# Moving an 8-byte tile so that activations and split weights start at multiples of 64 bytes

## The chip, the cores and the metric

One core of one Trainium2 chip runs one program, a transformer-like pair of blocks. The metric is the device time of one execution in microseconds (us). TensorE (PE) does the matmuls, its weight loads are the profile's PEld; VectorE is DVE, ScalarE is ACT, GpSimd is POOL, SyncE is SP. "Moving" is the operand that streams through TensorE (512 columns), "weights" is the 128x128 operand that is loaded before it.

## What is computed

Two blocks on x of shape 1 x 1024 x 1024. Block one: modulation from `c`, `h @ w_in`, three mixers (a state-space scan, a Fourier mix, window attention), `@ w_out`, then `(gelu(gate) * val) @ w_down` with a width-3 convolution after `w_up`. Block two: `u @ w_in_2`, four branches, a gated merge, `@ w_out_2`, then a squared-ReLU MLP. In cut form:

```python
h = rms_norm(x, g_pre_mix[l]) * (1.0 + sc_m) + sh_m
z = h @ w_in[l]
...
up = dwconv3(h @ w_up[l], conv_w[l], conv_b[l])
y = (jax.nn.gelu(gate) * val) @ w_down[l]
...
proj = jnp.einsum("btd,dp->btp", u, w_in[l])
hid = jnp.square(jax.nn.relu(jnp.einsum("btd,df->btf", u, w_up[l])))
m = jnp.einsum("btf,fd->btd", hid, w_down[l])
```

## The kernel before, in words

Activations lie transposed, channels on the 128 partitions and 1024 positions along each. The large products are done in split precision: every fp32 number is held as a high and a low part in type fp32r, and each product of a 128x128 weight block with 512 positions takes three matmuls, high by high, high by low, low by high. They are at lines 1698 to 1700 (function `mm`) for the plain products and at 1732 to 1734 (`pair_mm`) for two MLP stages in which pairs of panels are combined so that seven products do for eight; the merge of the four branches has the same three at 2078 to 2080. There are 2368 + 840 + 128 of each, so 10008 such matmuls of 128x512 in all.

Weights come as panels of 128x1024. A DMA brings a panel into the raw buffer `wraw` (line 1249), ACT copies it to the high part (helper line 2918), POOL subtracts to get the low part (helper line 3448). The split panel goes to one of four slots, and the slots are used in turn (`take_slot`: panel n goes to `(n + self.shift) % NW`, `NW` is 4). Three slots are one tile, `whl`, the fourth is a tile of its own, `whl4`, since it is allocated later:

```python
        A = sb("act", [P, 2, NK, T], F32R)
        wraw = sb("wraw", [P, NRAW, 1024])
        whl3 = sb("whl", [P, NW - 1, 2, 1024], F32R)
        sel = sb("sel", [P, 2])
...
        whl4 = sb("whl4", [P, 2, 1024], F32R)
        whl = [whl3[:, n, :, :] for n in range(NW - 1)] + [whl4[:, :, :]]
```

The moving operand is `act` (both parts of the normed activations) in the products with `w_in`, `w_out`, `w_up`; `hid1` or `hid2` (both parts of the MLP's hidden layer) in those with `w_down`; in the paired stages `act` and the sums `t12`, `t3`, `t3t` of halves of it. Profiles leave numbers out of tile names: `whl` stands for `whl` and `whl4`, `hid` for both hidden tiles, `t` for `t12` and `t3`. `sel` holds two columns and is read by 32 small matmuls in the first 50 us (lines 1756 and 1775).

The allocator puts a tile of 8 bytes per partition into 32 bytes. So the tiles lie as follows in each partition, by the built programs:

| tile | start before | over a multiple of 64 | start after | over a multiple of 64 |
|---|---|---|---|---|
| sel | 117728 | 32 | 19424 | 32 |
| act | 19424 | 32 | 19456 | 0 |
| wraw | 84960 | 32 | 84992 | 0 |
| whl (slots 0 to 2) | 93152 | 32 | 93184 | 0 |
| whl4 (slot 3) | 117760 | 0 | 117760 | 0 |
| hid1, hid2 | 158720 | 0 | 158720 | 0 |
| t12, t3, t3t | 125952, 191488, 158720 | 0 | the same | 0 |
| hz2, z3, wbl (the merge's operands) | 158720, 191488, from 224512 | 0 | the same | 0 |

All parts and blocks inside these tiles are at multiples of 512 bytes from their start (256 in the merge), so an operand has the remainder of its tile. Below, a matmul is **mixed** when its moving operand and its weights have different remainders (32 and 0, or 0 and 32), and **equal** when they have the same one. Counted from the program before:

| moving | weights | matmuls | kind |
|---|---|---|---|
| act | whl | 5160 | equal (32, 32) |
| act | whl4 | 1752 | mixed |
| hid1, hid2 | whl | 1248 | mixed |
| hid1, hid2 | whl4 | 384 | equal (0, 0) |
| t12, t3, t3t | whl | 840 | mixed |
| t12, t3, t3t | whl4 | 240 | equal (0, 0) |
| merge | merge | 384 | equal (0, 0) |

That makes 3840 mixed and 6168 equal ones. By time of start in the profiled execution, mixed and equal:

| stretch, us | mixed | equal |
|---|---|---|
| 0 to 420 | 120 | 441 |
| 420 to 552 | 144 | 379 |
| 552 to 670 | 240 | 248 |
| 670 to 940 | 513 | 660 |
| 940 to 1000 | 159 | 76 |
| 1000 to 1160 | 372 | 320 |
| 1160 to 1300 | 201 | 300 |
| 1300 to 2100 | 651 | 2469 |
| 2100 to 2400 | 641 | 651 |
| 2400 to 2700 | 733 | 563 |
| 2700 to the end | 66 | 61 |

Of the kernel before, what the change touches and what calls it, by code (L numbers as in the profile page):

```python
# [14 lines left out]
P = 128  # L15
# [19 lines left out]
class Marks:  # L35
# [35 lines left out]
    def mark(self, name, *key):  # L71
        return self.up(1, name, key)
# [4 lines left out]
    def done(self, name, *key):  # L77
        if self.known:
            return self.sem(name), self.value[(name, *key)]
        return self.sem(name), 0  # L80
# [1149 lines left out]
def build(nc, t):  # L1230
    ctx = ExitStack()
    with ctx:
        def sb(name, shape, dt=F32, c=ctx, side=None):
            return c.enter_context(nc.sbuf_tensor(name, list(shape), dt, side=side))
# [10 lines left out]
        gmod = sb("gmod", [P, 6, 8])  # L1245
        r8 = sb("r8", [P, NG])
        halfpi = sb("halfpi", [P, 1])
        A = sb("act", [P, 2, NK, T], F32R)
        wraw = sb("wraw", [P, NRAW, 1024])
        whl3 = sb("whl", [P, NW - 1, 2, 1024], F32R)  # L1250
        sel = sb("sel", [P, 2])


        cp = ExitStack()
# [88 lines left out]
        crow = X[1][:, 7, :]  # L1343
        XA = A[:, 0, :, :].bitcast(F32)
        arow = {j: tmp0[1 - j][:, :] for j in range(2)}
# [112 lines left out]
        def hid_view(name, q, h):  # L1458

            n = HID_SLOT[name][h]  # L1460
            if n > 5:
                return A[:, 1, 2 * (n - 6) + q, :]
            return H["f1"][:, n, q, :] if name == "f1" else hid[:, n, q, :]

        def part_view(s, t, q, e):

            if t == "t4":
                return A[:, q, e, 512:1024]
            if t == "t3":
                return TX3[:, 4 * q + e, :] if 4 * q + e < 6 else TX3t[:, 4 * q + e - 6, :]  # L1470
            return TX12[:, 0 if t == "t1" else 1, q, e, :]
# [6 lines left out]
        def moving(s, b, q, e):  # L1478

            if b[0] == "t":  # L1480
                return part_view(s, b, q, e)
            return A[:, q, e + (0 if b == "b11" else 4), HALF[b == "b22"]]

# [174 lines left out]
        def tensor(pe):  # L1658
# [12 lines left out]
            def mm(i, k0, k1):  # L1671
# [13 lines left out]
                for e in range(k0, k1):  # L1685
# [10 lines left out]
                    hi, lo = (whl[plan.slot[n]][:, q, cols[e]:cols[e] + 128] for q in range(2))  # L1696
                    x_hi, x_lo = (hid_view(g.kind[:2], q, k)[:, c] if down else A[:, q, k, c] for q in range(2))
                    pe.matmul(PSB[g.bank][:, :], hi, x_hi, start=e == 0, stop=False)  # L1698
# [394 lines left out]
        def vector(v):  # L2093
# [9 lines left out]
            def stt(out, a, s, b, op0, op1):  # L2103
                return v.scalar_tensor_tensor(out=out, in0=a, scalar=s, in1=b, op0=op0, op1=op1)  # L2104
# [55 lines left out]
            def apply(s, half):  # L2160
# [10 lines left out]
                for j in range(9):  # L2171
# [10 lines left out]
                    if j:  # L2182
                        i = j - 1
                        if shift is not None:
                            w.wait_ge(*done("apA", s, half, i))
                            stt(A[:, 1, i, c], tm[i % nt], shift(i), A[:, 0, i, c].bitcast(F32), ALU.add,
                                ALU.subtract).then_inc(*mark("apD", s, half, i))
# [1849 lines left out]
```

How the kernel before makes its waits and increments, by code:

```python
    def wait_ge(self, sem, value):  # L98
        if self.met.get(sem.name, 0) < value:
            self.met[sem.name] = value
            self.engine.wait_ge(sem, value)
# [1560 lines left out]
            def start():  # L1662
                w.wait_ge(*done("ones"))
# [7 lines left out]
            def mm(i, k0, k1):  # L1671
                g = tiles[i]
                n, down = g.n, g.kind in EVAC_ON_DVE
                w.wait_ge(*done("hi", n))
                w.wait_ge(*done("lo", n))
                if g.free and k0 == 0:
                    w.wait_ge(*done(*g.free))
                if down:
                    c0, k = chunk_of[g.kind][g.chunk]
                    cols, ks = [(g.pos * k + e) * 128 for e in range(k)], [c0 + e for e in range(k)]
                else:
                    ks = K_OUT if g.kind == "w_out" else range(8)
                    cols = [128 * k for k in ks]
                c = HALF[g.half]
                for e in range(k0, k1):
                    k = ks[e]
                    if down:
                        w.wait_ge(*hid_done(g.kind[:2], k))
                    elif g.kind == "w_out":
                        for d in mixed_done(k):
                            w.wait_ge(*d)
                    elif g.kind == "w_out2":
                        w.wait_ge(*split_done(g.half, k))
                    else:
                        w.wait_ge(*apply_done(APPLIED[g.kind], g.half, k))
                    hi, lo = (whl[plan.slot[n]][:, q, cols[e]:cols[e] + 128] for q in range(2))
```

## Time and profile before

| what | value |
|---|---|
| three runs | 2754.02, 2754.8, 2760.42 us; the median is 2754.8 |
| span of the profiled execution | 2751.9 us (the median of the runs is 2.9 us above it) |
| PE matmul busy | 2637.7 us, 96% of the span, 12542 records |
| DVE, ACT, POOL busy | 53%, 37%, 40% |
| granted TensorE clock | 0.93 to 420 us, then 0.99 to 1.00 to the last slice |

The profile gives no time of its own for the profiled execution beyond the span; the runs are timed around it. A matmul's duration is longer than the distance to the next start, since matmuls overlap, so rate is read from distances of starts, or from how many lie in a stretch.

### The profile page before, as it was taken

What the parts mean: (1) busy time and instruction counts of PE and PEld (TensorE: products, weight loads), DVE (VectorE), ACT (ScalarE), POOL (GpSimd) and SP (SyncE); (2) the same over time, 40 slices, a digit from 0 to 9 for tenths busy, and PEclk for the clock granted to TensorE, in tenths of its full rate; (3) what the DMA queues carried; (4) which work ended last, traced back from release to release, by engine and by line L of the source; (5) the groups of instructions that cost most, each with busy time, mean ns of one, the idle gap of its engine ahead of it and who ended that gap; (6) DMA issues with size and microseconds to landing.
All of it is one profiled execution on the core that took longest, in us unless ns stands there. A gap on an engine that the chain in (4) does not pass through costs nothing.

```text
span 2751.9 us, 31627 instructions
## 1 busy us (share of the span) xinstructions
PE 2637.7 (96%) x12542; PEld 2080.4 (76%) x12542; DVE 1465.6 (53%) x1881; ACT 1029.3 (37%) x1600; POOL 1091.4 (40%) x605
## 2 busy tenths in 40 slices
PE   6889989999999999999999999999999999999997
PEld 2657757777888788877777788888788788888885
DVE  5646658797777722276766422433457655322225
ACT  4413655455444511345454321211354434312112
POOL 1322114256656544442211142322353655534443
PEclk8999999999999999999999999999999999999998
DMA  6453247321222343241123122111324233433322
GB/s 247 178 146 101 78 173 285 113 81 66 81 84 83 112 146 126 84 145 59 54 68 109 54 88 67 58 48 48 137 91 153 77 115 104 149 118 128 115 77 85
DMA packets 109619, 297.92 MB, mean 108 GB/s; under 512 B 13344, under 2 KB 28192, under 8 KB 109472
## 3 DMA queue, kind: packets, MB, share of 16 engines
q1 hardware_dynamic: 102592, 275.36, 29.4%
q10 hardware_dynamic: 3456, 10.73, 1.0%
q0 software_dynamic: 3424, 9.81, 0.9%
q8 instruction: 100, 1.64, 0.2%
q14 instruction: 47, 0.39, 0.1%
HBM read 233.09 MB, written 62.76 MB: 108 GB/s over the span
## 4 chain that ended last, share of the span: by engine, by line
PE 71%; DVE 5%; ACT 1%; issue 1%; POOL 1%; DMA 1%; POOLq 0%; SPq 0%; DVEq 0%; ACTq 0%
PE ps L1698 16%; PE ps L1700 15%; PE ps L1699 15%; PE ps L1732 5%; PE ps L1734 5%; PE ps L1733 5%; PE pc L1732 1%; PE pc L1734 1%; PE pc L1733 1%; PE pss L2026 1%; PE pc L2078 1%; PE pc L2080 1%; PE pc L2079 1%; POOL whl L3448 1%; DVE pad L2104 0%
## 5 line engine op out<-in xcount | busy, mean ns | idle before, releaser
L3448 POOL TENSOR_TENSOR whl<-wraw,whl 128x1024 fp32r<-128x1024 f32 (+2 forms) x309 | 648.0, 2102 | 1242.0 <-ACT whl L2918 1241.8
L1698 PE MATMUL ps<-act,whl 128*128 128x512 f32 x1824 | 735.5, 403 | 34.7 <-DVE act L2098 9.2
L1699 PE MATMUL ps<-act,whl 128*128 128x512 f32 x1824 | 718.0, 394 | 0.0
L1700 PE MATMUL ps<-act,whl 128*128 128x512 f32 x1824 | 717.5, 393 | 0.0
L1698 PEld LDWEIGHTS ps<-act,whl 128*128 128x128 f32 x1824 | 344.9, 189 | 134.9 <-issue 43.3
L2918 ACT ACTIVATE whl<-wraw 128x1024 fp32r<-128x1024 f32 (+2 forms) x309 | 268.1, 869 | 461.9 <-PE ps L1700 372.6
L1700 PEld LDWEIGHTS ps<-act,whl 128*128 128x128 f32 x1824 | 344.9, 189 | 76.9
L1699 PEld LDWEIGHTS ps<-act,whl 128*128 128x128 f32 x1824 | 345.3, 189 | 75.7 <-issue 4.1
L2098 DVE TENSOR_TENSOR y<-y,ps 128x512 f32<-128x512 f32 x176 | 120.9, 687 | 365.6 <-PE ps L1700 365.4
L1698 PE MATMUL ps<-hid,whl 128*128 128x512 f32 x544 | 216.8, 399 | 4.4 <-DVE y L2502 4.3
L1700 PE MATMUL ps<-hid,whl 128*128 128x512 f32 x544 | 214.4, 394 | 0.0
L1699 PE MATMUL ps<-hid,whl 128*128 128x512 f32 x544 | 214.1, 394 | 0.0
L1732 PE MATMUL ps<-act,whl 128*128 128x512 f32 x360 | 141.2, 392 | 1.9 <-ACT rl L2918 1.3
L1734 PE MATMUL ps<-act,whl 128*128 128x512 f32 x360 | 140.9, 391 | 0.0
L1733 PE MATMUL ps<-act,whl 128*128 128x512 f32 x360 | 140.7, 391 | 0.0
L1698 PEld LDWEIGHTS ps<-hid,whl 128*128 128x128 f32 x544 | 102.1, 188 | 31.2 <-DVE y L2502 6.4
L1732 PE MATMUL ps<-t,whl 128*128 128x512 f32 x300 | 118.6, 395 | 3.0 <-ACT pad L2918 3.0
L1700 PEld LDWEIGHTS ps<-hid,whl 128*128 128x128 f32 x544 | 102.1, 188 | 24.5
L1699 PEld LDWEIGHTS ps<-hid,whl 128*128 128x128 f32 x544 | 102.0, 188 | 24.2 <-issue 0.7
L1734 PE MATMUL ps<-t,whl 128*128 128x512 f32 x300 | 118.3, 394 | 0.0
L2098 DVE TENSOR_TENSOR sgm<-sgm,pc 128x512 f32<-128x512 f32 x48 | 32.7, 681 | 154.5 <-PE pc L2080 154.5
L2918 ACT ACTIVATE sgm<-ps 128x512 f32<-128x512 f32 x46 | 27.5, 597 | 231.3 <-PE ps L1700 223.0
(402 smaller groups left out, 4206.1 us busy)
## 6 DMA issues: line engine op xcount, KB each, us to landing
wraw<-in_w_in SPq DMA_DIRECT2D x63, 512.0 KB, 3.4
wraw<-in_f1u SPq DMA_DIRECT2D x72, 256.0 KB, 2.8
wraw<-in_f2d SPq DMA_DIRECT2D x36, 512.0 KB, 3.4
wraw<-in_w_out SPq DMA_DIRECT2D x32, 512.0 KB, 3.4
x<-in_w_ada SPq DMA_DIRECT2D x32, 512.0 KB, 7.2
hid<-hscr SPq DMA_DIRECT2D x29, 512.0 KB, 6.6
xs<-y SPq DMA_DIRECT2D x24, 512.0 KB, 6.3
wraw<-in_f2u SPq DMA_DIRECT2D x48, 256.0 KB, 3.3
```

Source lines behind the costliest of these rows:

```text
L1698: pe.matmul(PSB[g.bank][:, :], hi, x_hi, start=e == 0, stop=False)
L1699: pe.matmul(PSB[g.bank][:, :], hi, x_lo, start=False, stop=False)
L1700: m = pe.matmul(PSB[g.bank][:, :], lo, x_hi, start=False, stop=e == len(ks) - 1)
L1732: pe.matmul(o[:, :], hi[:, c], x_hi, start=k in OPENS and e == 0, stop=False, skip_group_check=True)
L1733: pe.matmul(o[:, :], hi[:, c], x_lo, start=False, stop=False, skip_group_check=True)
L1734: m = pe.matmul(o[:, :], lo[:, c], x_hi, start=False, stop=e == 3, skip_group_check=True)
L2026: m = pe.matmul(PSS[:, h, n * 128:n * 128 + 128], ks[pr, cs_], qs[pr, cs_], start=True, stop=True)
L2078: pe.matmul(PSC[half][:, :], wh, yh, start=e == 0, stop=False)
L2079: pe.matmul(PSC[half][:, :], wh, yl, start=False, stop=False)
L2098: return v.tensor_tensor(out, a, b, op)
L2918: return a.activation(out, in_, func, **kw)
L3448: return g_.tensor_tensor(out, a, b, op)
```

## The change

`sel` is allocated before `act` instead of after `whl`. It takes the 32 bytes there, so `act`, `wraw` and `whl` start 32 bytes later, and everything allocated after them stays where it was. No size, no instruction and no order changes on any engine.

```diff
@@ -1245,10 +1245,10 @@
         gmod = sb("gmod", [P, 6, 8])
         r8 = sb("r8", [P, NG])
         halfpi = sb("halfpi", [P, 1])
+        sel = sb("sel", [P, 2])
         A = sb("act", [P, 2, NK, T], F32R)
         wraw = sb("wraw", [P, NRAW, 1024])
         whl3 = sb("whl", [P, NW - 1, 2, 1024], F32R)
-        sel = sb("sel", [P, 2])
 
 
         cp = ExitStack()
```

Since profiles leave tile numbers out, two pieces of PE's order (the same in both kernels) tell which slot a matmul reads. The first is where the panel in slot 2 ends and the one in slot 3 begins, 48 matmuls before the first merge matmul (L2078):

```order
5893 L1699 MATMUL ps0<-act,whl 128x512
5894 L1700 MATMUL ps0<-act,whl 128x512
5895 L1698 MATMUL ps1<-act,whl4 128x512
5896 L1699 MATMUL ps1<-act,whl4 128x512
...
5942 L1700 MATMUL ps0<-act,whl4 128x512
5943 L2078 MATMUL pc0<-z3 128x512
```

The second is in the last `w_down` product, where slot 3 with 48 matmuls stands between others, and 102 matmuls from slots 0 to 2 follow, the last 6 of them the first of a panel whose matmuls alternate between `hid2` and `act`:

```order
9166 L1700 MATMUL ps2<-hid2,whl 128x512
9167 L1698 MATMUL ps3<-hid2,whl4 128x512
...
9214 L1700 MATMUL ps2<-hid2,whl4 128x512
9215 L1698 MATMUL ps3<-hid2,whl 128x512
...
9316 L1700 MATMUL ps3<-hid2,whl 128x512
9317 L1698 MATMUL ps3<-act,whl 128x512
```

Nothing in either piece moves; only the addresses behind `act` and `whl` do.

## Rows read from the trace of the kernel before

**Rows 1.** The page: span, busy time, PE and its granted clock by slice.

```profile
span 2751.9 us, 31627 instructions
...
PE 2637.7 (96%) x12542; PEld 2080.4 (76%) x12542; DVE 1465.6 (53%) x1881; ACT 1029.3 (37%) x1600; POOL 1091.4 (40%) x605
...
PE   6889989999999999999999999999999999999997
...
PEclk8999999999999999999999999999999999999998
```

**Rows 2.** Waits of PE, the longest entry: waited for, us in total, times, longest us.

```profile
PE ps L1766 <- DMA adaw<-in_w_ada: 10.0, 9, 2.7
```

**Rows 3.** The page's groups: busy us, mean ns of one, idle before.

```profile
L1698 PE MATMUL ps<-act,whl 128*128 128x512 f32 x1824 | 735.5, 403 | 34.7 <-DVE act L2098 9.2
L1699 PE MATMUL ps<-act,whl 128*128 128x512 f32 x1824 | 718.0, 394 | 0.0
```

**Rows 4.** Timeline of PE, 1605 to 1628 us: start us, duration us, instruction.

```profile
1605.34 0.39 PE L1698 MATMUL ps<-act,whl 128*128 128x512 f32 x1
...
1616.22 0.39 PE L1698 MATMUL ps<-act,whl 128*128 128x512 f32 x1
...
1627.41 0.39 PE L2078 MATMUL pc<-z 128*128 128x512 f32 x1
```

**Rows 5.** Timeline of PE, 2385 to 2441 us.

```profile
2385.16 0.39 PE L1698 MATMUL ps<-hid,whl 128*128 128x512 f32 x1
...
2396.05 0.39 PE L1698 MATMUL ps<-hid,whl 128*128 128x512 f32 x1
...
2418.45 0.39 PE L1698 MATMUL ps<-hid,whl 128*128 128x512 f32 x1
...
2440.74 0.39 PE L1698 MATMUL ps<-hid,whl 128*128 128x512 f32 x1
```

**Rows 6.** Groups of PE, 2168.8 to 2171.2 us: t12 with whl.

```profile
L1732 PE MATMUL ps<-t,whl 128*128 128x512 f32 x4 | 1.6, 395 | 0.0
```

**Rows 7.** Groups of PE, 2248.7 to 2250.1 us: t3 with whl4.

```profile
L1732 PE MATMUL ps<-t,whl 128*128 128x512 f32 x3 | 1.2, 389 | 0.0
```

**Rows 8.** Windows of PE: stretch, length, busy (matmuls), clock, DMA share, GB/s.

```profile
0.00:420.00 420.00, 352.75 (x2233) 0.93 0.48 155
420.00:552.00 132.00, 129.18 (x565) 1.00 0.53 196
552.00:670.00 118.00, 113.84 (x490) 1.00 0.22 72
670.00:940.00 270.00, 269.94 (x1173) 1.00 0.23 82
...
1000.00:1160.00 160.00, 160.00 (x693) 1.00 0.32 115
1160.00:1300.00 140.00, 132.88 (x591) 0.99 0.30 104
...
2100.00:2400.00 300.00, 298.67 (x1293) 1.00 0.34 118
2400.00:2700.00 300.00, 300.00 (x1297) 1.00 0.29 105
```

**Rows 9.** The chain that ended last, by line, 560 to 680 us.

```profile
by line: POOL whl L3448 8.3%; PE ps L1732 7.8%; DVE pad L2098 7.7%; DVE pad L2104 7.6%; PE ps L1734 7.4%; PE ps L1733 7.3%; issue 5.5%; DVE cv L2104 5.0%; DMA hscr<-pad 4.7%; DVE act L2098 4.4%; DVE x L2104 4.0%; DVE late L2098 3.8%; ACT pa
```

**Rows 10.** The same, 1160 to 1300 us.

```profile
by line: PE ps L1698 17.3%; PE ps L1700 16.5%; PE ps L1699 16.4%; DMA E<-in_hmask 3.8%; issue 3.7%; POOL whl L3448 3.5%; DVE pad L2104 3.0%; PE pc L1983 2.5%; DVE act L2098 2.4%; DMA wraw<-in_w_in 2.4%; ACT act L2918 2.3%; DVE z L2098 2.2%;
```

**Rows 11.** Timeline of POOL, 1607 to 1648 us: low parts of four successive panels.

```profile
1607.16 2.39 POOL L3448 TENSOR_TENSOR whl<-wraw,whl 128x1024 fp32r<-128x1024 f32 x1 [8.29 <-ACT whl L2918]
1618.04 2.41 POOL L3448 TENSOR_TENSOR whl<-wraw,whl 128x1024 fp32r<-128x1024 f32 x1 [8.49 <-ACT whl L2918]
...
1629.24 2.41 POOL L3448 TENSOR_TENSOR whl<-wraw,whl 128x1024 fp32r<-128x1024 f32 x1 [2.67 <-ACT whl L2918]
...
1645.62 2.41 POOL L3448 TENSOR_TENSOR whl<-wraw,whl 128x1024 fp32r<-128x1024 f32 x1 [9.11 <-ACT whl L2918]
```

## The prediction

> **What bounds the kernel now.** I read the page first. PE's matmuls are busy in 2637.7 of 2751.9 us, no other engine in more than 53%, and after the first slices every slice of PE is a 9 at a granted clock of 9 or 10 tenths, that is at 2.4 GHz [rows 1]. Its waits are few: the longest entry comes to 10 us over the whole program [rows 2]. So the time is the number of matmuls times the distance between two starts, wherever PE is on the chain. The next question is that distance. The page's groups cannot give it, because a matmul's duration (394 or 403 ns [rows 3]) overlaps the next one. From starts it can be had, and here the program holds an experiment of its own: the weight slot changes from panel to panel while everything else stays.
>
> With `act` moving, 48 matmuls on a panel in slot 2 (remainders 32 and 32) take 1616.22 - 1605.34 = 10.88 us, which is 226.7 ns each; the next 48, the same line and tiles but slot 3 (32 and 0), take 1627.41 - 1616.22 = 11.19 us, 233.1 ns each [rows 4]. That alone could be something about slot 3. But with `hid` moving it is the other way round: slot 3 (0 and 0) takes 2396.05 - 2385.16 = 10.89 us for 48, 226.9 ns each, and the 96 from slots 0 and 1 (0 and 32) take 22.40 us, 233.3 ns each [rows 5]. The paired stage agrees by durations, which grow with the distance: `t12` with `whl` has 395 ns, `t3` with `whl4` 389 [rows 6, 7]. So neither tile is slow by itself. A matmul costs some 6.5 ns more (233.3 - 226.8) when moving operand and weights lie at different remainders over 64 bytes, and both equal kinds, 32/32 and 0/0, have the same speed.
>
> **The change, term by term.** It adds and removes no instruction. It makes all 10008 of these matmuls equal, at 0 and 0.
>
> 1. The mixed matmuls get faster: 3840 x 6.5 ns = 25.0 us.
>
> 2. A surcharge where the kind changes. Between 2418.45 and 2440.74 us a panel in slot 2 and one in slot 3 are used with `hid` and `act` in turns of six, so 48 of 96 matmuls are mixed. They should take 96 x 230.05 ns = 22.08 us and take 22.29 [rows 5]: 0.2 us, or 4.4 ns per mixed one, on top. Over the four long stretches with PE alone the windows tell the mean. 670 to 940, 1000 to 1160, 2100 to 2400 and 2400 to 2700 us are 1030 us with 1028.6 busy and 1173 + 693 + 1293 + 1297 matmuls [rows 8], less one at most edges that is counted on both sides: 4453. At 226.75 ns they would take 1009.7 us; the 2259 mixed ones add 14.7; 1.4 us are idle; 4.2 us remain, 1.9 ns per mixed matmul. Scaled to 3840 that is 7.1 us. I take all of it, as no kind changes after the edit; if it has another cause it stays, so the bounds are 0 and 7.1. Terms 1 and 2 make 32.1 us, or 8.4 ns per mixed matmul.
>
> 3. What is not passed on. In 0 to 420 us PE is busy 84% [rows 8] and waits for transfers and small steps; 120 mixed ones are worth 1.0 us, and I take it as lost. In 420 to 552 us PE is busy 98%, 144 are worth 1.2 us, half lost. In 552 to 670 us 240 are worth 2.0 us, but PE's three lines are only 22.5% of the chain there, beside POOL's splits and DVE's `pad` work [rows 9]: 1.6 lost. In 1160 to 1300 us 201 are worth 1.7 us with PE 53% of the chain [rows 10]: 0.8 lost. For the scattered waits elsewhere I add 0.2. Together 4.2 us. The bounds are 0 (all passed on) and about twice this, 8.
>
> 4. The other engines. POOL's low-part subtraction is 2.39, 2.41, 2.41 and 2.41 us on four successive panels [rows 11], one of which goes to `whl4` while it reads `wraw` at remainder 32; the target's remainder makes no difference there. I take nothing for DVE, ACT and POOL, and should a write get slower by some ns, PE covers it: POOL sat idle 8 us and more before three of those four. The raw panels' transfers end early enough for that too. If this cover were gone, a late split would show as waits of PE on `whl`, of which it has none near the 10 us of its longest entry now [rows 2]. `sel` keeps its remainder.
>
> Sum: 25.0 + 7.1 - 4.2 = 27.9 us. From the span of 2751.9 that gives 2724.0; the median of the runs is 2.9 above the span, so 2726.9, said as 2727 us, 1.0% less. A difference of 0.3% (8.3 us) is about what a measurement of this kernel can tell from none.
>
> **A rule that speaks against it.** The rows show a distance that depends on both operands' addresses. The Trainium skill, page "SBUF — State Buffer", section "SBUF: two separate sides", gives TensorE its own port and, in the table under "A bandwidth-pool intuition that's wrong", a second independent read port for weight loads; its specifications name lines of 16 bytes. By that a start 32 bytes off is still on a line's edge and the two reads cannot meet, and the time would stay at 2754.8. The two crossing stretches [rows 4, 5] disagree with it, by 6.5 ns a matmul.
>
> **Rivals.**
>
> A. The remainder is not the cause. The two slots could differ in something else that goes with it, such as how far apart the operands lie, and both tiles that are now at 32 would simply keep their mixed partners slow. Then nothing changes: 2754.8. Against it: act, hid and t cross over with the slot, far apart in address, and after the edit every operand has the relation that `hid` and `whl4` have now. For it: remainders have been seen in two values only, and each with few tiles. The page's rule above ends at the same time. Chance 5%.
>
> B. Real on PE, but eaten by others. If a faster PE finds DVE and the splits late in the paired stages too, where DVE is busiest, half of terms 1 and 2 goes: 2754.8 - 16 = 2738.8, say 2739. For it: the chain of 560 to 680 us. Against it: 670 to 940 us has the same paired work and PE is busy 269.94 of 270 us [rows 8]. Chance 12%.
>
> C. Slower. While PE waits, the granted clock can fall: in 0 to 420 us, busy 84%, it is 0.93, which is 59 us at 1.2 GHz, and in stretches of 96% and more it is 1.00 [rows 8]. If shorter matmuls leave more gaps, gaps bring falls and each us at 1.2 GHz costs half a us. To end above no change by 0.3% this must cost 28 + 8 = 36 us, so 72 us more at half clock, over twice what there is now; the result would be 2763. [...] Chance 1%.
>
> **How the numbers follow.** The forecast has 82%. Its own range is from all passed on (2754.8 - 32.1 = 2722.7, and 2 us below that for a run like the fastest and for a last matmul rate a little under 226.7) to no surcharge gained and doubled losses (25.0 - 8 = 17: 2737.8). With B and some room for the median of few runs, which reached 5.6 us above itself once, the range is 2719 to 2741; A and C, 6%, and some ends of the others are outside. Faster by over 0.3% are the forecast and B, 94% with a little of A's doubt taken off: 0.93. Within 0.3%: 0.05. Slower: 0.02.
>
> **What would show it.** In the profile after, 48 matmuls on any slot take 10.88 to 10.90 us with any moving tile; the durations are 389 ns everywhere, with L1699's mean under 392; 300 us of pure matmuls hold about 1323 instead of 1293 to 1297; PE's busy total falls by 30 us or more, while its waits rise by some 4. DVE, ACT and POOL keep their busy times. The prediction is wrong if panels of slot 3 still differ from the others, if all matmuls are now at 233 ns (then 32/32 was the good case, and equal at 0 fails with the new neighbours), or if PE's idle time grows by more than 8 us.

## The result and the profile after

| | median, us | runs | against before, 95% interval |
|---|---|---|---|
| before | 2756.9 | 2754.02 to 2760.42 | |
| changed | 2732.6 | 2729.13 to 2737.33 | 0.991 [0.9896, 0.9925] |
| predicted | 2727 | 2719 to 2741 | |

The kernel is 24 us faster (27.9 forecast). The forecast was worked out from the 2754.8 us of three runs; with a fourth run the median of the kernel before is 2756.9. The page of the changed kernel:

```profile
span 2727.3 us, 31627 instructions
...
PE 2613.6 (96%) x12542; PEld 2082.2 (76%) x12542; DVE 1460.0 (54%) x1881; ACT 1028.4 (38%) x1600; POOL 1095.9 (40%) x605
...
PEclk8999999999999999999999999999999999999998
```

Beside [rows 1] the span is 24.6 us shorter and PE's busy time 24.1, with the same granted clock in every slice; the other engines keep theirs within 6 us. PE's unbusy time is the same: 2751.9 - 2637.7 = 114.2 and 2727.3 - 2613.6 = 113.7. The two groups of [rows 3], busy us and mean ns of one:

```profile
L1698 PE MATMUL ps<-act,whl 128*128 128x512 f32 x1824 | 732.3, 401 | 35.1 <-DVE act L2098 8.3 <-POOL act L3448 6.6 <-DVE act L2104 5.3
L1699 PE MATMUL ps<-act,whl 128*128 128x512 f32 x1824 | 714.5, 392 | 0.0
```

The timeline of PE (start us, duration us) answers to [rows 4]: the panel in slot 2 begins at 1594.86, the one in slot 3 at 1605.74, and the merge at 1616.70. The next panel in slot 3 is from 1665.66 to 1676.54.

```profile
1594.86 0.39 PE L1698 MATMUL ps<-act,whl 128*128 128x512 f32 x1
...
1605.74 0.44 PE L1698 MATMUL ps<-act,whl 128*128 128x512 f32 x1
...
1616.70 0.39 PE L2078 MATMUL pc<-z 128*128 128x512 f32 x1
...
1665.66 0.39 PE L1698 MATMUL ps<-act,whl 128*128 128x512 f32 x1
...
1676.54 0.39 PE L2078 MATMUL pc<-z 128*128 128x512 f32 x1
```

Slot 2 still takes 10.88 us for 48 matmuls, 226.7 ns each. Slot 3 takes 10.96 the first time, where its first matmul was held up a little (0.44 instead of 0.39 us), and 10.88 the second, where it took 233 ns a matmul before. The same for [rows 5], slot 3 and then slots 0 and 1 with `hid`, and then the panels that alternate between `hid` and `act`:

```profile
2367.44 0.39 PE L1698 MATMUL ps<-hid,whl 128*128 128x512 f32 x1
...
2378.32 0.39 PE L1698 MATMUL ps<-hid,whl 128*128 128x512 f32 x1
...
2400.08 0.39 PE L1698 MATMUL ps<-hid,whl 128*128 128x512 f32 x1
...
2421.84 0.39 PE L1698 MATMUL ps<-hid,whl 128*128 128x512 f32 x1
```

48 matmuls in 10.88 us, 96 in 21.76 and 96 in 21.76: all 226.7 ns. The alternating stretch had 22.29 us, so the surcharge there is gone too. Windows of PE (length, busy and number of matmuls), beside [rows 8]:

```profile
552.00:670.00 118.00, 112.19 (x488) 1.00 0.21 72
670.00:940.00 270.00, 269.64 (x1190) 1.00 0.24 84
1000.00:1160.00 160.00, 159.92 (x708) 1.00 0.34 120
2100.00:2400.00 300.00, 298.61 (x1309) 1.00 0.32 113
```

15 to 17 more matmuls fit into each of the three long stretches. In 552 to 670 us there are 488 where there were 490: no gain there.

### The profile page after: what moved, and what is told of

Its sections match the earlier page's. It is cut to its first block, busy times and chain, and to the rows that moved or that the text cites. A ratio compares the mean times of both kernels' runs of the same rounds, so it can differ in the third digit from the quotient of the medians.

```text
span 2727.3 us, 31627 instructions
## 1 busy us (share of the span) xinstructions
PE 2613.6 (96%) x12542; PEld 2082.2 (76%) x12542; DVE 1460.0 (54%) x1881; ACT 1028.4 (38%) x1600; POOL 1095.9 (40%) x605
## 4 chain that ended last, share of the span: by engine, by line
PE 70%; DVE 5%; POOL 2%; ACT 1%; issue 1%; DMA 1%; SPq 0%; POOLq 0%; DVEq 0%; ACTq 0%
PE ps L1698 15%; PE ps L1700 15%; PE ps L1699 15%; PE ps L1732 5%; PE ps L1734 5%; PE ps L1733 5%; PE pc L1732 1%; PE pc L1734 1%; PE pc L1733 1%; PE pss L2026 1%; POOL whl L3448 1%; PE pc L2078 1%; PE pc L2080 1%; PE pc L2079 1%; DVE pad L2104 0%
## 5 line engine op out<-in xcount | busy, mean ns | idle before, releaser
L1698 PE MATMUL ps<-act,whl 128*128 128x512 f32 x1824 | 732.3, 401 | 35.1 <-DVE act L2098 8.3
L1699 PE MATMUL ps<-act,whl 128*128 128x512 f32 x1824 | 714.5, 392 | 0.0
L1700 PE MATMUL ps<-act,whl 128*128 128x512 f32 x1824 | 714.3, 392 | 0.0
L1698 PEld LDWEIGHTS ps<-act,whl 128*128 128x128 f32 x1824 | 344.8, 189 | 132.1 <-issue 38.5
L1700 PEld LDWEIGHTS ps<-act,whl 128*128 128x128 f32 x1824 | 344.9, 189 | 73.4
L1699 PEld LDWEIGHTS ps<-act,whl 128*128 128x128 f32 x1824 | 345.4, 189 | 72.5 <-issue 4.1
L1698 PE MATMUL ps<-hid,whl 128*128 128x512 f32 x544 | 214.4, 394 | 0.4
L1700 PE MATMUL ps<-hid,whl 128*128 128x512 f32 x544 | 212.2, 390 | 0.0
L1699 PE MATMUL ps<-hid,whl 128*128 128x512 f32 x544 | 212.0, 390 | 0.0
L1732 PE MATMUL ps<-act,whl 128*128 128x512 f32 x360 | 140.6, 390 | 3.4 <-ACT whl L2918 1.5
L1698 PEld LDWEIGHTS ps<-hid,whl 128*128 128x128 f32 x544 | 102.4, 188 | 24.5 <-DVE y L2502 1.8
L1732 PE MATMUL ps<-t,whl 128*128 128x512 f32 x300 | 117.0, 390 | 2.9 <-ACT pad L2918 2.9
L1699 PEld LDWEIGHTS ps<-hid,whl 128*128 128x128 f32 x544 | 102.3, 188 | 22.0 <-issue 1.0
L1700 PEld LDWEIGHTS ps<-hid,whl 128*128 128x128 f32 x544 | 102.2, 188 | 21.4
```

The costliest lines, as they stand in the source:

```text
L1699: pe.matmul(PSB[g.bank][:, :], hi, x_lo, start=False, stop=False)
L1700: m = pe.matmul(PSB[g.bank][:, :], lo, x_hi, start=False, stop=e == len(ks) - 1)
L1732: pe.matmul(o[:, :], hi[:, c], x_hi, start=k in OPENS and e == 0, stop=False, skip_group_check=True)
```

## The experiments

All kernels differ from the changed one only in where tiles lie, so they compute the same. Where an edit adds lines ahead of the matmuls, their line numbers are one or two higher; the text says which is which. **d** is the start of the moving operand less the start of the weights.

### Is it the remainder over 64?

All at 32, from the order of before:

```diff
         whl3 = sb("whl", [P, NW - 1, 2, 1024], F32R)
         sel = sb("sel", [P, 2])
+        sb("pad32", [P, 8])
```

> The order of before (act at 32 over a multiple of 64) and a further tile of 32 bytes behind sel, so that whl4, hid, t12, t3 and the merge's tiles lie at 32 too: all 10008 matmuls equal, none at a multiple of 64. If it is the relation of the two operands that counts, this runs like the changed kernel, 24 to 28 us under before (about 2730), and every matmul starts 226.7 ns after the last. If starts at multiples of 64 are what is fast, it is slower than before, up to 10008 x 6.5 ns = 65 us over the changed kernel (2797).

Measured: 2750.7 us, 0.9984 of before [0.9974, 0.9994]. This is neither of the two numbers expected. All pairs have equal remainders over 64, and yet it gains 6 us and not 24. This was the first sign that the reading of the traces was too narrow.

`sel` between `act` and `wraw`:

```diff
-        sel = sb("sel", [P, 2])
         A = sb("act", [P, 2, NK, T], F32R)
+        sel = sb("sel", [P, 2])
         wraw = sb("wraw", [P, NRAW, 1024])
```

> sel stands between act and wraw: act at 32, all weights, hid and sums at 0. By the relation, 6912 matmuls (all with act) are mixed at 233.3 ns and the 3096 others equal at 226.7: 6912 x 6.6 = 46 us over the changed kernel and some us for changes of kind, so about 2780, 20 to 25 us over before. If slot 3 itself, or the number of tiles at multiples of 64, decides, it lies between before and the changed kernel (2732 to 2757), since more tiles are at 0 than before.

Measured: 2769.5 us, 1.0049 of before [1.0032, 1.0065]. More tiles lie at multiples of 64 than before, and it is slower: slot 3 or the number of round addresses is ruled out as the cause. The rise over the changed kernel is 37 us where 46 and more were expected.

64 bytes behind `act`:

```diff
         A = sb("act", [P, 2, NK, T], F32R)
+        sb("pad64", [P, 16])
         wraw = sb("wraw", [P, NRAW, 1024])
```

> 64 bytes are put behind act, so act is at 0 and everything behind it at 64 over a multiple of 128. If only the remainder over 64 counts, it runs like the changed kernel (about 2730). If the remainder over 128 counts, 6912 matmuls are mixed and it runs near 2780.

Measured: 2766.7 us, 1.0035 of before [1.0022, 1.0048]. Every tile starts at a multiple of 64, and the kernel is 34 us slower than the changed one. So "a multiple of 64" is not what makes it fast. The groups of line 1699 (1700 in the last kernel), with 32 and with 64 bytes between `act` and the weights:

```profile
L1699 PE MATMUL ps<-act,whl 128*128 128x512 f32 x1824 | 726.3, 398 | 0.0
...
L1699 PE MATMUL ps<-hid,whl 128*128 128x512 f32 x544 | 213.0, 391 | 0.0
```

```profile
L1700 PE MATMUL ps<-act,whl 128*128 128x512 f32 x1824 | 725.5, 398 | 0.0
...
L1700 PE MATMUL ps<-hid,whl 128*128 128x512 f32 x544 | 212.7, 391 | 0.0
```

In both, the `act` group's mean is 6 ns above the changed kernel's 392 while `hid`, which kept its relation to the weights, has 391.

### Ladders of distances

Since slots change from panel to panel, one kernel can hold four distances for `act` and four for `hid`. In the near ladder the slots are 32 bytes apart:

```diff
-        whl3 = sb("whl", [P, NW - 1, 2, 1024], F32R)
+        whl3 = sb("whl", [P, 6168], F32R)
...
-        whl4 = sb("whl4", [P, 2, 1024], F32R)
-        whl = [whl3[:, n, :, :] for n in range(NW - 1)] + [whl4[:, :, :]]
+        whl4 = sb("whl4", [P, 2048], F32R)
+        sb("padC", [P, 8])
+        whl = [t_.rearrange("p (q c) -> p q c", q=2) for t_ in [whl3[:, 2056 * n:2056 * n + 2048] for n in range(NW - 1)] + [whl4[:, 0:0 + 2048]]]
```

> A ladder read in the trace, not meant to be fast. act at 0; weight slots 0 to 3 at 0, 32, 64 and 96 over a multiple of 512; hid, sums and merge tiles at 128. With d for start of the moving operand less start of the weights, over a multiple of 512, act gives d of 0, -32, -64, -96 and hid gives 128, 96, 64, 32. If d alone decides (both tiles' own places do not), the spacing seen so far must come back: 0 -> 226.7 ns, -32 -> 233.3, -64 -> 233.3, 32 -> 233.3, 64 -> 229.0; -96, 96 and 128 are new. If the places themselves decide, at least one of these five comes out otherwise by over 1 ns.

PE's timeline in the near ladder. The plain triple (the three matmuls of one product, L1698 to L1700 in the changed kernel) begins at L1699 here. `act` with slots at 32, 64 and 96 begins at 1603.07, 1614.27 and 1625.47, and with the one at 0 at 1642.19; the merge begins at 1636.70 and 1653.09:

```profile
1603.07 0.39 PE L1699 MATMUL ps<-act,whl 128*128 128x512 f32 x1
...
1614.27 0.40 PE L1699 MATMUL ps<-act,whl 128*128 128x512 f32 x1
...
1625.47 0.39 PE L1699 MATMUL ps<-act,whl 128*128 128x512 f32 x1
...
1636.70 0.40 PE L2079 MATMUL pc<-z 128*128 128x512 f32 x1
...
1642.19 0.39 PE L1699 MATMUL ps<-act,whl 128*128 128x512 f32 x1
...
1653.09 0.39 PE L2079 MATMUL pc<-z 128*128 128x512 f32 x1
...
2390.89 0.39 PE L1699 MATMUL ps<-hid,whl 128*128 128x512 f32 x1
...
2401.90 0.39 PE L1699 MATMUL ps<-hid,whl 128*128 128x512 f32 x1
...
2413.10 0.40 PE L1699 MATMUL ps<-hid,whl 128*128 128x512 f32 x1
...
2424.26 0.40 PE L1699 MATMUL ps<-hid,whl 128*128 128x512 f32 x1
```

48 matmuls each: 11.20, 11.20 and 11.23 us for d of -32, -64 and -96, 10.90 for 0. With `hid` at 128 (the last four rows), 11.01 us for d = 64, 11.20 for 32 and 11.16 for 128: d of 64 is less dear than of -64.

The far ladder has the same edit and 128 bytes ahead of `whl3`:

```diff
+        sb("padA", [P, 32])
         whl3 = sb("whl", [P, 6168], F32R)
```

> The same ladder with the slots at 128, 160, 192 and 224, hid at 256: act gives d of -128, -160, -192, -224, hid gives 128, 96, 64, 32 once more from other places. If d alone decides, the four of hid repeat those of the near ladder within 0.3 ns. If what decides repeats over 128 bytes, -128 has 226.7 ns and -160 has 233.3; if it repeats over 256 only, -224 has what 32 has (233.3) and -192 what 64 has (229.0).

The rows of the far ladder, where the plain triple begins at L1700: `act` with the slot at 160, and a later panel with the one at 192; then `hid` at 256 with slots at 192 and 224.

```profile
1605.15 0.40 PE L1700 MATMUL ps<-act,whl 128*128 128x512 f32 x1
...
1616.35 0.40 PE L1700 MATMUL ps<-act,whl 128*128 128x512 f32 x1
...
1674.66 0.39 PE L1700 MATMUL ps<-act,whl 128*128 128x512 f32 x1
...
1685.64 0.39 PE L2080 MATMUL pc<-z 128*128 128x512 f32 x1
...
2391.37 0.40 PE L1700 MATMUL ps<-hid,whl 128*128 128x512 f32 x1
...
2402.37 0.40 PE L1700 MATMUL ps<-hid,whl 128*128 128x512 f32 x1
```

11.20 us for d = -160, 10.98 for -192, and 11.00 for `hid` with d = 64. The last is the near ladder's 11.01 again from other places, and -192 has what 64 has: what decides repeats over 256 bytes, and not over 128 (over 128, -192 would be -64 and have 233.3 ns).

The fine ladder takes slots 0 to 2 at 4, 16 and 48:

```diff
-        whl3 = sb("whl", [P, NW - 1, 2, 1024], F32R)
+        whl3 = sb("whl", [P, 6156], F32R)
...
-        whl = [whl3[:, n, :, :] for n in range(NW - 1)] + [whl4[:, :, :]]
+        whl = [t_.rearrange("p (q c) -> p q c", q=2) for t_ in [whl3[:, n:n + 2048] for n in (1, 2052, 4108)] + [whl4[:, :, :].rearrange("p q c -> p (q c)")]]
```

> Small shifts: act at 0, slots 0 to 2 at 4, 16 and 48, slot 3 and hid at 64. act gives d of -4, -16, -48, -64, hid gives 60, 48, 16, 0. If the reads meet in units of 32 bytes or more, -4 and -16 are near 226.7 or between it and 233.3; if any start off the other's costs, all but hid with slot 3 are near 233. -64 must be 233.3 and 0 must be 226.7 again.

`act` with the slot at 4, then with the one at 16, each up to the next merge:

```profile
1638.30 0.39 PE L1698 MATMUL ps<-act,whl 128*128 128x512 f32 x1
...
1649.45 0.39 PE L2078 MATMUL pc<-z 128*128 128x512 f32 x1
...
1652.20 0.39 PE L1698 MATMUL ps<-act,whl 128*128 128x512 f32 x1
...
1663.40 0.39 PE L2078 MATMUL pc<-z 128*128 128x512 f32 x1
```

11.15 us for d = -4, 232.3 ns each, and 11.20 for -16: one element off on this side already costs nearly all. The near, far and fine ladders took 2771.6, 2772.2 and 2767.3 us, one run each, beside 2756.5 of before.

The means over all stretches in which at least ten matmuls before had the same relation, worked out from the starts in the traces of before, of the changed kernel and of seven experiments, by d over 256 (what d is above or below the nearest multiple of 256):

| d | 0 | 16 | 32 | 48 | 60 | 64 | 96 | 128 | -96 | -64 | -48 | -32 | -16 | -4 |
|---|---|---|---|---|---|---|---|---|---|---|---|---|---|---|
| ns | 226.7 | 227.8 | 233.3 | 232.2 | 233.4 | 228.8 | 233.4 | 232.4 | 234.3 | 233.3 | 233.3 | 233.3 | 232.4 | 232.3 |

The sign counts at the small distances too: with the moving operand 16 bytes above the weights a matmul costs 1.1 ns more than at 0, with it 16 below 5.7.

The first experiment is explained by it: in all-at-32, `act` to `whl4` has d = 448 over 512 (480 less 32), which is -64 over 256 and has 233.4 ns; but `hid` and `t` to `whl` have +64 (32 less 480) and fell from 233.3 to 228.8 ns: 2088 x 4.5 = 9.4 us at most, 6 measured.

### Which weights, own or next?

> Each weight slot gets 32 bytes between its high and its low part, so the low parts alone are at 32, all else is at 0: a third of the matmuls (3208) is mixed. If a stream is slowed by the weights that are loaded during it (the next matmul's), the long distance is from the start of L1699 to that of L1700, which has the low part, and L1700 to L1698 is short. If it is slowed by its own weights, the long distance is from L1700 to L1698. In time 3208 x 6.6 = 21 us over the changed kernel, and more if a change of kind at every matmul costs something (up to 4 ns for each of some 6400, 26 us).

The edit was 32 bytes between high and low part within each slot (`whl3 = sb("whl", [P, NW - 1, 2064], F32R)` and the like for `whl4`). Measured: 2775.1 us, 1.0071 [1.0056, 1.0087], 42 us over the changed kernel. As a test it failed: the pitch of the slots became 8256 bytes, so the high parts had distances of their own. It was made again with all high parts ahead of all low ones:

```diff
-        whl3 = sb("whl", [P, NW - 1, 2, 1024], F32R)
+        whl3 = sb("whl", [P, 2 * 3080], F32R)
...
+        sb("padB", [P, 48])
         whl4 = sb("whl4", [P, 2, 1024], F32R)
-        whl = [whl3[:, n, :, :] for n in range(NW - 1)] + [whl4[:, :, :]]
+        w3_ = whl3[:, :].rearrange("p (q c) -> p q c", q=2)
+        whl = [w3_[:, :, 1024 * n:1024 * n + 1024] for n in range(NW - 1)] + [whl4[:, :, :]]
```

> The test of own against next weights without the mixed slot places of the first try: in slots 0 to 2 the high parts are at 0 and the low parts at 32, act at 0. Three matmuls in turn have high, high and low weights. If a stream is slowed by the next matmul's weights, which are loaded during it, then L1699 to L1700 (named one line further down here) is the long distance, near 233 or more, and the others are near 227. If its own weights slow it, L1700 to L1698 is the long one. Slot 3, hid and the sums are at 256: if 256 apart is as good as 0, act with slot 3 and hid with slots 0 to 2's high parts are at 226.7.

The plain triple is L1700 (high weights), L1701 (high) and L1702 (low) here. Groups of PE in 1601 to 1608 us, `act` with slot 0, busy us and mean ns of one:

```profile
L1701 PE MATMUL ps<-act,whl 128*128 128x512 f32 x11 | 4.4, 400 | 0.0
L1702 PE MATMUL ps<-act,whl 128*128 128x512 f32 x11 | 4.3, 389 | 0.0
L1700 PE MATMUL ps<-act,whl 128*128 128x512 f32 x10 | 4.0, 395 | 0.0
```

The matmul with equal weights of its own but the shifted low part next is the long one, 400 ns; the one that uses the shifted weights has the short 389. The ends of matmuls are modelled in the profile, so the starts are the better evidence, and they agree: over all such triples with `act` on slots 0 to 2 (some 1300), the mean distance from L1701 to L1702 is 238.0 ns, from L1702 to L1700 228.6, and from L1700 to L1701 232.6. The timelines of PE and of its weight loads show when the weights of L1702 come:

```profile
1611.11 0.40 PE L1701 MATMUL ps<-act,whl 128*128 128x512 f32 x1
1611.11 0.19 PEld L1702 LDWEIGHTS ps<-act,whl 128*128 128x128 f32 x1
1611.34 0.39 PE L1702 MATMUL ps<-act,whl 128*128 128x512 f32 x1
```

They are loaded in the first 0.19 us of the matmul before, which is the slow one. So a stream is slowed by the weights that are loaded during it. The load itself is no longer: 188 ns on average in the kernel before, whether the matmul over it is equal or mixed. The 395 ns of the third matmul, and its 232.6 ns to the next start, were not expected: the disturbance reaches further than that one stream, and no run shows why. Five triples on the timeline of the same run,

```profile
1610.17 0.40 PE L1700 MATMUL ps<-act,whl 128*128 128x512 f32 x1
...
1613.67 0.40 PE L1700 MATMUL ps<-act,whl 128*128 128x512 f32 x1
```

take 3.50 us, 15 x 233 ns: as much as if all matmuls were mixed, though one of three weights is. `act` with slot 3, d = -256, has a mean of 226.7 ns between starts. The kernel took 2761.5 us in its one run.

### Timed against each other

The changed kernel once more:

> The changed kernel once more, beside the next three on one chip. 2725 to 2736 us, 0.8 to 1.0% under before.

256 bytes between `act` and the rest:

```diff
         A = sb("act", [P, 2, NK, T], F32R)
+        sb("pad256", [P, 64])
```

> The changed kernel with 256 bytes behind act: act stays at 0, all else is 256 further, so every matmul with act has d = -256 over 512. If what decides repeats over 256 bytes, it is within 0.1% of the changed kernel and all spacings are 226.7 ns. If it repeats over 512 or not at all, the 6912 matmuls with act are slower and it comes near 2765.

`act` 64 above a multiple of 256, the rest at one:

```diff
+        sb("padlow", [P, 16])
         A = sb("act", [P, 2, NK, T], F32R)
+        sb("padhigh", [P, 48])
```

> act 64 bytes above a multiple of 256 and all else at one, so d = +64 for the 6912 matmuls with act, where the 64-apart run had -64 (2766.7 us). If d alone decides, and with its sign, these are at 228.8 ns instead of 233.3: 2.1 ns x 6912 = 15 us over the changed kernel, less some 2 for the first 700 us, about 2745, and 20 us under the run with -64. If the sign does not matter, near 2766.

The mixers' tiles from 32 to 0 over 256:

```diff
         alt = sb("alt", [P, 1], c=pu)
+        sb("padF", [P, 56], c=pu)
```

> The changed kernel with 224 bytes behind alt, which brings FA, vrow, sc, dg and pt of the mixers from 32 to 0 over a multiple of 256. They meet about 500 further matmul passes between 150 and 450 us. At 6.6 ns each this would be 3 us at most, and since a faster PE gained nothing up to 700 us, no difference to the changed kernel (within 0.1%). If the start of the program did pass gains on, 1 to 3 us less.

| kernel | median, us | against before, 95% interval |
|---|---|---|
| changed again | 2733.7 | 0.9914 [0.9901, 0.9927] |
| act 256 apart | 2732.3 | 0.9912 [0.9898, 0.9926] |
| act 64 above | 2748.5 | 0.9972 [0.996, 0.9984] |
| mixers aligned | 2735.6 | 0.9926 [0.9913, 0.994] |

The first line confirms the result. 256 bytes apart is as good as 0 in the time too. +64 is 18 us better than -64 (2766.7) and 15 us worse than 0, as 6912 x 2.1 ns had it; the sign counts. Aligning the mixers' tiles brings nothing that can be measured. No kernel beats the changed one by more than the scatter of its runs, and 0 over 256 is the lowest of all distances tried.

### How much is passed on

The first and last start of a line (after the three durations) mark places in the program. L1732 begins with the first paired stage, `hid` at L1698 with the product after it. In the kernel before:

```profile
L1732 PE MATMUL ps<-act,whl x360: 387/389/477, 590.7 to 2373.0; 128*128 128x512 f32 x180
...
L1698 PE MATMUL ps<-hid,whl x544: 387/396/799, 943.6 to 2730.6; 128*128 128x512 f32 x182
```

In the changed kernel, and in its second run:

```profile
L1732 PE MATMUL ps<-act,whl x360: 389/389/473, 590.7 to 2355.6; 128*128 128x512 f32 x180
...
L1698 PE MATMUL ps<-hid,whl x544: 387/389/1203, 939.7 to 2705.9; 128*128 128x512 f32 x182
```

```profile
L1732 PE MATMUL ps<-act,whl x360: 387/389/473, 593.1 to 2360.6; 128*128 128x512 f32 x180
...
L1698 PE MATMUL ps<-hid,whl x544: 387/389/799, 942.2 to 2710.8; 128*128 128x512 f32 x182
```

Up to 590.7 us nothing was gained, and the same kernel came there at 590.7 and 593.1, so the start of the program varies by more than was to be gained in it. Between the marks before took 352.9 us, the changed kernel 349.0 and 349.1. From the first mark to the last start it is 2139.9, 2115.2 and 2117.7 us: 24.7 and 22.2 gained, all of it behind 590 us.

## Why the prediction was right, and where not

**The whole.** The mechanism was right: the distance between starts on PE depends on how the two operands lie to each other, and the change made it short everywhere. The rule given for it was wrong, one term was twice too large, and the time came out inside the range all the same. Of the 5.7 us between 2726.9 and 2732.6, 2.1 come from the median of before (2754.8 then, 2756.9 with a fourth run) and 3.6 from the sum (27.9 forecast, 24.3 measured).

**The bound.** Right: with the same clock and the same idle time in the profile, the distances between starts made the difference. Split by the distance from each of the 10008 starts to the next start on PE, the two traces give:

| | before | changed | difference |
|---|---|---|---|
| under 300 ns, to another of the 10008 | 9688 of them, 2228.6 us | 9674, 2197.1 us | 28.4 us less for the same number |
| all others | 319, 157.0 us, or 84.6 above 227.1 ns each | 333, 163.8 us, or 88.2 above | 3.6 us more |
| the rest of the span | 366.2 us | 366.4 us | 0.2 us more |

28.4 - 3.6 - 0.2 is the 24.6 us by which the span fell. The first line is what terms 1 and 2 had at 32.1, the other two what term 3 had at 4.2.

**Term 1, 25.0 us.** The size was right and its rule wrong. Equal matmuls are at 226.7 ns and the 3840 mixed ones went there from 233.3. But "different remainders over 64" was the wrong name for mixed. The step that failed is the sentence in which the two crossing stretches were read as showing what remainders do: [rows 4, 5] have only d of 0, 32 and -32 over 256, and every rule that tells 0 from these fits them. That the number came out right all the same was luck of the layout: the change happens to bring all the large tiles to multiples of 256 and most to multiples of 512, so d is 0 over 256 for all of them; all-at-32 and 64-apart satisfy the stated rule and are 18 and 34 us slower. Rival A was near this doubt ("remainders have been seen in two values only") but drew the wrong conclusion from it, that the change would then do nothing.

**Term 2, 7.1 us.** This is the term that was mis-sized: about half of it came. Over the three long stretches above and 2400 to 2650 us (1105 matmuls after, 1082 before), 978.2 us of busy time hold 4312 matmuls less 4 counted twice: 227.06 ns each, against 230.97 before. 0.4 ns is still over 226.7, which is 3.6 us for 10008. So some 3.5 of the 7.1 was not from changes of kind. The split above says the same: 28.4 less the 25.0 of term 1 leaves 3.4. The traces also show where the true part sat: in the kernel before, the first two distances behind a change from mixed to equal weights are 231.8 and 232.5 ns on average, where 226.7 is usual, while the distances behind the opposite change average what mixed ones do. The trace of the changed kernel shows what the part that stayed looks like: the panel at 1605.74 us, d = 0 throughout, has a late first matmul (0.44 us) and takes 10.96 us instead of 10.88. That a late start costs spacing afterwards fits this panel; no run tested it.

**Term 3, 4.2 us lost.** The sum was about right: 3.6 + 0.2 = 3.8 in the split above. Place by place it was too hopeful early (552 to 670 us passed on nothing), and the profile's idle time did not grow, where 4 us had been expected: the loss hides in matmuls that wait while the one before still counts as busy. The size is no better known than the waits repeat: the second run of the changed kernel has the same short distances, but 348 others with 172.6 us, 9.0 us more above 227.1 ns each than before. A slow-down is not passed on in full either: 6912 mixed matmuls with `act` 32 off cost 37 us over the changed kernel, not 46.

**Term 4, nothing.** Right. POOL's low parts in the changed kernel:

```profile
1596.68 2.39 POOL L3448 TENSOR_TENSOR whl<-wraw,whl 128x1024 fp32r<-128x1024 f32 x1 [8.29 <-ACT whl L2918]
1607.56 2.41 POOL L3448 TENSOR_TENSOR whl<-wraw,whl 128x1024 fp32r<-128x1024 f32 x1 [8.49 <-ACT whl L2918]
```

They are as long as in [rows 11], now with `wraw` moved as well.

**Rivals.** B (half eaten by others) is wrong in size: 24.6 of 28.4 us came through. C did not occur, the granted clock is as before.

**The signs.** The prediction named PE's busy total falling by 30 us or more, and it fell by 24.1; this was the same term 2 too large. It named waits of PE rising by some 4 us, and they did not in the profile's idle time. The median durations did go to 389 ns and the mean of L1699 to 392. Of the signs of being wrong, none came.

## What to carry to other kernels

When matmuls run back to back with new weights each time, look at the distance of starts by tile: here it is 226.7 ns where moving operand and weights lie a multiple of 256 bytes apart and up to 234 elsewhere, and a few bytes of padding settle it. All runs had fp32r matmuls of 128x512 with 128x128 weights; other types and sizes were not tried. Before a pattern in a trace is turned into a rule, list which values of the quantity it has shown; two values that cross over prove a relation, not its period.

## What the runs showed of the hardware

- The distance between two 128x512 fp32r matmuls depends on where the moving operand lies against the weights that are loaded meanwhile, by up to 7.6 ns (3.4%), and on nothing of their own places: d = 0 gives 226.7 ns at remainders 0, 32, 64 and 96 over 128 alike. It repeats over 256 bytes, is not symmetric (64: 228.8, -64: 233.3; 16: 227.8, -16: 232.4) and is there at one element (-4: 232.3).
- The Trainium skill, page "SBUF — State Buffer", section "A bandwidth-pool intuition that's wrong (but worth ruling out)", has a second independent read port for weight loads. By it no such dependence would be there; the runs show one of 6.6 ns, so the measurement decides.
- The Trainium skill, page "TensorE: Matmul & The Clock Gate", section "Architectural detail: the array is 16× 32×32, not 1× 128×128", says that TensorE pulls a weight load ahead of matmuls in flight. The run with shifted low parts agrees: the load of L1702 starts with the matmul before it, at 1611.11 us, and most of the cost stands there, 400 ns against 389.
- That the two reads meet in SBUF is inferred from this; no run shows the place.
